# Overflow blocks of a mixture of experts run as a pipeline with one counter per step, and expert matrices loaded in longer runs

## The reference, cut to what matters

```python
def _moe(h, gates, w1, w3, w2):
    y = jnp.zeros_like(h)
    for e in range(N_EXPERTS):                     # 16
        a = jax.nn.silu(h @ w1[e]) * (h @ w3[e])   # w1, w3: 1024 x 512
        y = y + gates[..., e:e + 1].astype(h.dtype) * (a @ w2[e])   # w2: 512 x 1024
    return y
```

## Time and profile before

| | |
|---|---|
| Median of 3 runs (lowest to highest) | 1519.93 us (1517.79 to 1527.5) |
| The profiled execution | 1532.7 us, its span 1531.1 us |
| Busy share of the span: PE, weight loads on PE, DVE, ACT, POOL | 76%, 33%, 23%, 15%, 13% |
| Mean granted clock of TensorE | 0.878 |
| DMA over the span | 338.15 MB, 221 GB/s |
| The mixture's stretches in that span | 427 to 892 us (layer 0), 1185 to 1494 us (layer 1) |

### The profile page before, as it was taken

How to read it: one execution, slowest core, us unless ns; L and a number is a source line. 1 busy time by engine, 2 the same in 40 slices (tenths; PEclk the granted TensorE clock), 3 DMA queues, 4 the chain that set the end, 5 groups by cost and what they waited for, 6 DMA issues and landing times.

```text
span 1531.1 us, 15042 instructions
## 1 busy us (share of the span) xinstructions
PE 1161.2 (76%) x4674; PEld 502.6 (33%) x4675; DVE 357.9 (23%) x691; ACT 227.0 (15%) x474; POOL 205.9 (13%) x249
## 2 busy tenths in 40 slices
PE   4799699999767767676877724999892877778770
PEld 1345466344222222222322312455242322223230
DVE  0320228254200001000101048315242010010114
ACT  0111218201110000100111100114210111011110
POOL 1300000024200000000000126200022000010003
PEclk9899799998788879889999966999895899898995
DMA  9813830817824544626999974141675799699952
GB/s 310 314 55 108 320 121 1 316 42 246 309 77 129 193 144 131 199 62 217 377 380 384 384 266 170 65 155 55 222 257 193 254 377 379 225 383 383 350 192 89
DMA packets 143847, 338.15 MB, mean 221 GB/s; under 512 B 8652, under 2 KB 10828, under 8 KB 143812
## 3 DMA queue, kind: packets, MB, share of 16 engines
q1 hardware_dynamic: 125780, 282.03, 51.1%
q0 software_dynamic: 13456, 41.96, 8.6%
q10 hardware_dynamic: 4576, 13.71, 2.2%
HBM read 306.47 MB, written 31.20 MB: 221 GB/s over the span
## 4 chain that ended last, share of the span: by engine, by line
PE 54%; SPq 12%; DMA 12%; DVE 10%; issue 7%; POOL 3%; ACT 2%; ACTq 1%; POOLq 0%; DVEq 0%
PE PS L1519 16%; PE PS L1343 13%; SPq L465 10%; PE PS L1531 7%; DMA W<-in_moe_w 6%; PE PS L1454 5%; PE PS L1303 2%; PE PS L1409 1%; PE PS L1292 1%; PE PS L1314 1%; DMA W<-in_w_ada 1%; DVE EX L1208 1%; DMA xg_rows<-H,DEST 1%; PE PS L1525 1%; DMA scrap<-C 1%
## 5 line engine op out<-in xcount | busy, mean ns | idle before, releaser
L1519 PE MATMUL PS<-W,XT 128*64 128x512 f32 x1376 | 351.4, 669 | 91.7 <-issue 42.4
L1531 PE MATMUL PS<-W,AT 128*64 128x512 f32 x688 | 179.5, 669 | 60.3 <-issue 41.2
L1343 PE MATMUL PS<-W,XT 128*128 128x512 f32 (+1 forms) x544 | 221.0, 568 | 2.7 <-ACT RB L713 1.8
L1519 PEld LDWEIGHTS PS<-W,XT 128*64 128x64 f32 x1376 | 117.0, 154 | 316.3 <-issue 307.1
L1208 DVE COPY EX<-PS 128x512 f32<-128x512 f32 x43 | 29.7, 691 | 485.0 <-PE PS L1519 485.0
L1343 PEld LDWEIGHTS PS<-W,XT 128*128 128x128 f32 x544 | 105.3, 195 | 113.4 <-issue 111.1
L1531 PEld LDWEIGHTS PS<-W,AT 128*64 128x64 f32 x688 | 56.6, 151 | 154.2 <-issue 141.4
L871 ACT ACTIVATE XT<-PS 128x512 f32<-128x512 f32 x34 | 20.3, 597 | 504.7 <-PE PS L1506 504.7
L643 POOL DMA_DIRECT2D y_rows<-H x64 | 34.2, 534 | 413.6 <-DVE H L1241 385.9
L1454 PE MATMUL PS<-W,XT 128*128 128x512 f32 x192 | 83.1, 593 | 0.0
L1506 PE MATMUL PS<-C,H 64*128 64x64 f32 x360 | 32.8, 234 | 51.2 <-DMA H<-xg_rows 33.3
(11 more groups left out here) (178 smaller groups left out, 943.5 us busy)
## 6 DMA issues: line engine op xcount, KB each, us to landing
W<-in_moe_w SPq DMA_DIRECT2D x96, 2048.0 KB, 20.6
W<-in_w_ada SPq DMA_DIRECT2D x24, 2048.0 KB, 10.5
W<-in_w_in SPq DMA_DIRECT2D x8, 2048.0 KB, 20.1
H<-xg_rows POOLq DMA_DIRECT2D x47, 256.0 KB, 6.5
xg_rows<-X ACTq DMA_DIRECT2D x1, 8192.0 KB, 29.2
W<-in_w_out SPq DMA_DIRECT2D x4, 2048.0 KB, 7.9
y_rows<-H POOLq DMA_DIRECT2D x64, 128.0 KB, 5.2
y_rows<-X ACTq DMA_DIRECT2D x1, 4096.0 KB, 38.5
```

Source lines behind the costliest of these rows:

```text
L1343: mm = pe.matmul(ps[:, 0:cw], XT[:, k, P * t:P * t + P], w[:, k, :], start=(k == 0), stop=(k == KD - 1))
L1519: mm = pe.matmul(PS[ROWS * n:ROWS * n + ROWS, p, :], XGT[:, p, k, :], moe_up(3 * p + n)[:, k, :], start=(k == 0), stop=(k == KD - 1), tile ...
L1531: mm = pe.matmul(PS[ROWS * n:ROWS * n + ROWS, 6 + p, :], ATX[:, p, k, :], moe_down(3 * p + 2)[:, k, 512 * n:512 * n + 512], start=(k == 0) ...
```

## The change

Six things change. (1) The overflow block has a semaphore for each of nine steps, each of which counts blocks, so a step waits for what it needs and no longer for all that comes before. PE turns an expert's first overflow rows right after its main `up`, and the next block's rows right after a block's `up`. These rows are copied to a buffer of their own (`XGTO`). PE's wait for the copy of the result moves ahead of the next `down`. (2) ACT, PE, POOL and DVE follow that order; PE and ACT read the counts earlier. (3) Partition p gets rows 8p to 8p + 7 of w1 and w3 (4p to 4p + 3 of w2), so its share is one run of 16 KB. The columns of the other operand have to be taken in the same order: the transposes read every eighth column of the rows and every fourth of `EX`. (4) The four base counts are set at the program's start. (5) The parameter loads of layer 1 come after the scatter and the first row loads. (6) ACT does one silu on two numbers at the start of each round.

```diff
@@ SP
-                src = src.rearrange("(k p) n -> p k n", p=P) if isinstance(at, int) else \
-                    src.rearrange("o (k p) n -> p (o k) n", p=P)
+                src = src.rearrange("(p k) n -> p k n", p=P) if isinstance(at, int) else \
+                    src.rearrange("o (p k) n -> p (o k) n", p=P)
...
-                                    sp.wait_ge(spill_step[L], spilt * SPILL + 1)
+                                    wait_apart(sp, spill_done[L]["down"], spilt + 1)
@@ POOL, spill
-                            v = (before + (j - 1)) * SPILL + 1
-                            wait_apart(pool, spill_step[L], v + 1)
+                            n = before + j
+                            wait_apart(pool, spill_done[L]["rows"], n)
                             with pool.If(cnt > (j + 1) * ROWS):
                                 spill_load(L, before + j)
-                            wait_apart(pool, spill_step[L], v + SPILL)
+                            wait_apart(pool, spill_done[L]["out"], n + 1)
@@ POOL, experts
-                if L == 0:
-                    pool.wait_ge(const_in, 16)
-                    for n, written in enumerate([*y_written, *spill_written]):
-                        pool.dma_start(scrap[n:n + 1, :], IDENT[0:1, :]).then_inc(written, 16)
-                        pool.wait_ge(written, 16)
...
                 rows_in(0, 0)
                 rows_in(1, 1)
-                pool.wait_ge(spill_step[L], 1)
+                if L + 1 < DEPTH:
+                    params(L + 1)
+                if L == 0:
+                    for written in (*y_written, *spill_written):
+                        pool.wait_ge(written, 16)
+                pool.wait_ge(meta_ready, L + 1)
@@ ACT
+                    nc.scalar.activation(T2[:, 0:1], T2[:, 1:2], ACT.Silu)
                     for p in range(2):
+                        cnt, before = spill_counts(2 * i + p)
+                        with act.If(cnt > ROWS):
+                            spill_turned(p, before + 1)
                         rows_turned(1 - p, i + (mb[5 - p] + 1 + p))
                         act.wait_ge(bank_full[2 + p], i + (mb[2 + p] + 1))
...
@@ PE
+                    turned = src.rearrange("t (d k) -> t k d", k=KD)
                     for k in range(KD):
-                        mm = pe.transpose(PS[:, 4 + p, ROWS * k:ROWS * k + ROWS], src[:, P * k:P * k + P],
-                                          IDENT[0:ROWS, 0:ROWS])
+                        mm = pe.transpose(PS[:, 4 + p, ROWS * k:ROWS * k + ROWS], turned[:, k, :], IDENT[0:ROWS, 0:ROWS])
...
-                        mm = pe.transpose(PS[:, 2 + p, P * n:P * n + P], EX[:, p, P * n:P * n + P], IDENT)
+                        mm = pe.transpose(PS[:, 2 + p, P * n:P * n + P],
+                                          EX[:, p, :].rearrange("t (f k) -> t k f", k=FE // P)[:, n, :], IDENT)
...
                         up(p).then_inc(bank_full[p], 1)
+                        cnt, before = spill_counts(2 * i + p)
+                        with pe.If(cnt > ROWS):
+                            spill_rows(p, before + 1)
                         if p == 0:
                             rows(1, i * 16 + 16 * (9 * L + 1), i + mb[5])
...
+                        wait_apart(pe, done["out"], before + 1)
                         down(p).then_inc(bank_full[6 + p], 1)
-                        spill(i, p)
+                        with pe.If(cnt > ROWS):
+                            wait_apart(pe, bank_free[6 + p], i + (mb[6 + p] + 1))
+                            with pe.Fori(1, 2 * T) as j:
+                                with pe.If(cnt > j * ROWS):
+                                    n = before + j
+                                    pe.wait_ge(done["turned"], n)
+                                    up_spilt(p).then_inc(done["up"], 1)
+                                    with pe.If(cnt > (j + 1) * ROWS):
+                                        spill_rows(p, before + (j + 1))
+                                    pe.wait_ge(done["both"], n)
+                                    turn_act(p).then_inc(done["act"], 1)
+                                    pe.wait_ge(done["product"], n)
+                                    wait_apart(pe, done["out"], n)
+                                    down(p).then_inc(done["down"], 1)
+                                with pe.Else():
+                                    pe.nop()
+                            pe.nop()
```

More of the change, by code:

```diff
@@ L392, in backbone @@
         spill_written = [sem(f"spill_written{L}") for L in range(DEPTH)]
-        spill_step = [sem(f"spill_step{L}") for L in range(DEPTH)]
+        meta_ready = sem("meta_ready")
+        SP_STEPS = ("rows", "turned", "up", "both", "act", "gate", "product", "down", "out")
+        spill_done = [{name: sem(f"spill_{name}{L}") for name in SP_STEPS} for L in range(DEPTH)]
         LAYER_DMAS = 5
@@ L672, in _ @@
             load_sgu_w(0)
+            pool.wait_ge(const_in, 16)
+            for n, written in enumerate([*y_written, *spill_written]):
+                pool.dma_start(scrap[n:n + 1, :], IDENT[0:1, :]).then_inc(written, 16)
             for L in range(DEPTH):
@@ L872, in rows_turned @@
                         .then_inc(bank_free[4 + p], 1)
[L874 to L885, removed]
-                                act.wait_ge(step, v + 5)
-                                nc.scalar.activation(GU[:, p, :, :], turned_gate(p), ACT.Silu).then_inc(step, 1)
-                            with act.Else():
-                                act.nop()
-                        act.nop()
@@ L892, in _, with spill_counts, spill_turned @@
-                act.wait_ge(spill_step[L], 1)
+                done = spill_done[L]
+                def spill_counts(e):
+                    return (act.value_load(META[0:1, L, 0, bass.ds(e, 1)], min_val=0, max_val=512),
+                            act.value_load(META[0:1, L, 1, bass.ds(e, 1)], min_val=0, max_val=16))
+                def spill_turned(p, n):
+                    act.wait_ge(done["rows"], n)
+                    nc.scalar.activation(XGTO, PS[:, 4 + p, :].rearrange("p (k s) -> p k s", k=KD), ACT.Copy)\
+                        .then_inc(done["turned"], 1)
@@ L896, in _ @@
                         rows_turned(1 - p, i + (mb[5 - p] + 1 + p))
                         act.wait_ge(bank_full[2 + p], i + (mb[2 + p] + 1))
-                        nc.scalar.activation(GU[:, p, :, :], turned_gate(p), ACT.Silu).then_inc(silu_done, 1)
-                        spill(2 * i + p, p)
+                        gate(p, silu_done)
+                        with act.If(cnt > ROWS):
+                            with act.Fori(1, 2 * T) as j:
+                                with act.If(cnt > j * ROWS):
+                                    n = before + j
+                                    with act.If(cnt > (j + 1) * ROWS):
+                                        spill_turned(p, before + (j + 1))
+                                    act.wait_ge(done["act"], n)
+                                    gate(p, done["gate"])
+                                with act.Else():
+                                    act.nop()
+                            act.nop()
@@ L1222, in spill @@
                             with dve.If(cnt > j * ROWS):
-                                v = (before + (j - 1)) * SPILL + 1
-                                both(p, (step, v + 3), step)
-                                product(p, (step, v + 6), step)
+                                n = before + j
+                                both(p, (done["up"], n), done["both"])
+                                product(p, (done["gate"], n), done["product"])
                                 dve.wait_ge(spill_written[L], (before + (j - 1)) * 32 + 16)
-                                dve.wait_ge(step, v + 8)
-                                dve.tensor_copy(YS, PS[:, 6 + p, :]).then_inc(step, 1)
+                                dve.wait_ge(done["down"], n + 1)
+                                dve.tensor_copy(YS, PS[:, 6 + p, :]).then_inc(done["out"], 1)
                             with dve.Else():
```

67 lines of the change are left out of this document (32 added, 35 removed).

## The result

The changed kernel takes 1514.17 us (median of 12 runs, 1509.57 to 1526.55), the kernel before 1526.05 us beside it (12 runs, 1517.79 to 1533.67). The ratio is 0.9925 with an interval of 0.990 to 0.995: 0.75% faster, less than the 1% that counts here as a change. I had forecast 1477 us, a ratio of 0.972, with 1439 to 1514 as the range and 0.79 for faster by over 1%. The prediction was wrong: the gain is under 1%, and the time lies just above its range.

The account below looks back on a forecast made before the run. PE's order of steps was taken to bound layer 0's overflow stage, weight DMA the other mixture stretches; -1.6 - 23.0 - 18.8 = -43.4 from 1532.7 gave 1489.3, times 0.9917: 1477 us, range 1439 to 1514.

Parts of the forecast that it names:

- Waits that come in its place: PE, asking earlier, waits for first overflow rows of seven experts in both layers: +19 us, bounds 0 and +33.
- the gap before `up`: PE's gap between the last overflow block and the next expert: -3.0 us for each of eight, -24; bounds -10 and -40.
- the five terms: Gap, row waits, clock, columns and runs, taken as independent; squares added gave 38 and 37 us, so 1439 to 1514.
- The clock term: PE's granted clock in layer 0's overflow stage rises from 0.86 to 0.90 with fewer gaps: -10 us, bounds 0 and -30.
- Strided columns: PE's turns of rows and `EX` slow by 0.35 us a block in some 23 blocks: +8 us, bounds 0 and +31.
- Longer runs: Weights in 16 KB runs at 420 GB/s: -0.97 us an expert over 19.4 experts, -18.8; bounds 0 and -37.6.
- Scrap writes: Layer 0's scatter no longer starts behind the last scrap write: -1.6 us and no more, the router's result being late next.
- (c): Rival: strided loads and row waits at their upper bounds eat the pipeline's gain, +37: 1514 us, no change that counts; chance 0.14.
- (a): Rival: overflow stage at full clock and long runs at 449 GB/s: -82, 1438 us; chance 0.16.
- (b): Rival: the long runs bring nothing, the rate may be the memory's: -24.6, 1495 us; chance 0.13.
- (d): Rival: slower, long runs stream worse in the three full-DMA stretches, 309 GB/s: +86, 1580 us; chance 0.07.

Follow-up runs that it names:

- pipeline with short runs: The changed kernel with the weight runs (2 and 4 KB) and the transposes' neighbouring columns of before, all else as changed: 1509.61 us, 0.9886.
- loads-ahead kernel: The changed kernel, but POOL loads the next overflow block as soon as the last has been turned, whichever expert it belongs to: 1449.05 us, 0.9499.
- the runs alone: The kernel before with the 16 KB runs and the transposes of every eighth and fourth column, nothing else: 1515.99 us, 0.9939.
- The last version: The loads-ahead kernel with PE's bank wait moved ahead of the overflow block's down and three first weight loads held until the scatter landed: 1438.51 us, 0.9452.

## Why the prediction was wrong

**The step that failed** is "Waits that come in its place": +19 us in seven places, measured 47.3. The mechanism was named, and the places were right; the size was not, by 28.3 us. For expert 1 the forecast had PE ask 10 us after DVE's copy and the rows land 13.0 after it. Measured from the end of that copy at 478.61: PE asks 7.0 us after it (485.65) and the rows land some 16 after it (PE starts at 494.81). Both sides were off by 3 us.
- PE came earlier because the gap before `up` was smaller than assumed, 0.68 us in place of 3, and `up` was at full clock. That was a gain in another term: the gap gave -28.8 us in this stage for -18. I had called the five terms independent and added their squares. These two were one quantity: whatever PE gains before it asks for the rows, it loses again in the wait, because the load's time is set by POOL. The net of the two was forecast at -3 us for the stage and measured +14.4.
- The rows landed later because the load took longer than 6.8 us: 8.9 us in the median, and 9.7 from this one's issue at 485.11 us to PE's start. The pipeline with short runs has 6.4 and the kernel before with long runs alone 9.0, so the 16 KB runs beside it are the cause. The forecast knew this as a bound (2 us more each) and left it out of the sum.

**The wait's second price was missed.** A wait costs its length and then a slow stretch: 0.55 granted around and behind 9.17 us of idle time, `down` 6.34 us for 3.65. Taking away 47.3 us of waits brought 65. The clock term itself, -10, came out, but by luck: strided turns added 4.4 us in the row groups (12.0 to 16.4) and about 1.4 in the turns of `EX` (9.8 to the 11.2 us of the loads-ahead kernel), so with PE's busy time down by 5.1 the rest is about -11. It is a difference of two large numbers: `up` gained 21.4 us, `down` lost 9.3. And the mean clock stood still at 0.85, for the 0.90 forecast.

**Strided columns.** A row group takes 1.10 us for 0.68, a group of `EX` 0.75 for 0.66: together +0.51 a block, for +0.35. PE's weight loads (ns, minimum, median, maximum):

```profile
L1520 PEld LDWEIGHTS PS<-C,H x360: 181/202/212, 429.1 to 1468.3; 64*128 64x128 f32 x180
```

It took 138 ns before. The Trainium skill (Advanced Engine Details and Errata, SBUF Cachelines) had warned of a penalty for a new line on each access; the trace agrees that there is one, of 64 ns a load, and not the doubling that I took as the upper bound.

**Longer runs.** 143,847 packets became 74,216, so the runs did grow. The rate in the full stretch, in 40 slices from 747 to 867 us, beside the earlier trace rows:

```profile
GB/s 426 422 442 285 401 426 407 433 362 333 426 421 431 438 339 365 437 426 426 392 296 421 426 422 441 375 307 437 431 425 434 330 367 426 431 426 410 306 396 415
```

Of the 40 slices 23 now show 421 to 442 GB/s, better than the 420 forecast, but the dips for row traffic are still there. An expert takes 17.15 us (seven from the `up` at 747.08 us to that at 867.14) instead of 17.85 (seven from 752.12 to 877.08): -0.70, for -0.97. An estimate from the Trainium skill's price per packet (DMA: Bandwidth & Descriptors, Why small descriptors are slow) had given -0.51; the measured gain lies between the two. Over 19.4 experts the shortfall of 0.27 is some 5 us.

**Scrap writes.** The scatter did start earlier, by 0.5 us (396.40), but its wait grew from 13.2 to 19.24 us, and the first transposes come 2.2 us later, not 1.6 earlier. The longer scatter is mostly the long runs' doing: the runs alone show it without the early bases (19.17 us), the pipeline with short runs has 15.25. The late start is not theirs alone: that pipeline starts as late (429.33 us), since what its scatter gains, its first row load loses. What part of the 2.2 us the moved parameter loads or the early bases have stays open. I had named the router's result as what is late next, and had not asked what the weights in flight do to the scatter and the first row load.

**The sum.** Of the 25.2 us by which the span missed (-18.2 for -43.4), the row waits make +28.3, the start of layer 0 +3.8 and the runs +5; the larger gain at the gap takes back 11.6 over both layers (42.4 - 6.8 = 35.6, for 24). Together 25.5: the rest is small misses of both signs that cancel. The time missed by 37 us (1514.17 for 1477), 12 more than the span: I had scaled the sum by 0.9917 from a profiled execution that lay over its median, and the changed kernel's lies at its median. Unscaled, the sum was 1489.3 us.

**The rivals.** (c), to which I gave 0.14, named this time (1514 us), to the microsecond by luck, and half of its mechanism: the row waits went past their upper bound (47.3 us for 33), the strided columns stayed below theirs (0.51 x 23 = 12 us for 31). The last version's 1438.51 us is (a)'s figure, but not by (a)'s way: it took three more edits, and the slices of the changed kernel stop at 442 GB/s, short of 449. (b) and (d) fell with the rates above.

Not tried: the early counter bases and the moved parameter loads by themselves, and shorter empty turns of the loops.

## What to carry to other kernels

When a step is moved ahead in the program of an engine that works in order, work out when its input arrives as well: the load has to be issued earlier by as much as the request moves, or the request has to stay behind the work that does not need it; else that work waits too. A gain just ahead of a wait whose end another engine sets is no gain; count the two as one term. And if an edit puts more bytes in flight in each transfer, look up which small transfers share those DMA engines and who waits for them.

## What was not expected of the hardware

- Weight transfers in 16 KB runs slow the small transfers beside them: an overflow load of 256 KB lands 8.9 us after its issue for 6.4 with 2 and 4 KB runs, and layer 0's scatter ends at 425.5 us for 421.6. With three of six weight matrices held back it ends at 409.9. The first row load behind the scatter goes the other way, 3.48 us for 7.65 with short runs.
- After the five waits of 7.6 to 9.9 us in layer 0 PE's next steps run slow, `down` 5.6 to 6.5 us for 3.65: a granted clock of 0.55 from 492 to 506 us, around and behind the 9.17 us wait, where 1.00 is granted from 484 to 496 us to the same steps without it.
- One silu at the head of each round takes 20 table loads of 1.28 us out of the mixtures of the loads-ahead kernel (36 to 16), and 16.5 us out of its time.
